# Moving the steps of the sample's key list on TensorE, and two top-k masks of the prompt into the attention

## What is computed

```python
def indexer_select(qi, wi, ki, q_pos, k_pos, n_top):
    s = jnp.einsum('bqhd,bld->bqhl', qi, ki) * IDX_DIM ** -0.5
    score = jnp.einsum('bqh,bqhl->bql', wi * IDX_HEADS ** -0.5, jax.nn.relu(s))
    score = jnp.where((k_pos[None, :] <= q_pos[:, None])[None], score, -jnp.inf)
    return lax.top_k(score, n_top)[1]
```

## Time and profile before

| | us |
|---|---|
| median of 3 runs | 1556.02 (1554.37 to 1559.13) |
| profiled execution | 1564.1 |
| its span | 1562.4 |
| PE busy | 1503.9 (96%) |
| DVE busy | 925.2 (59%) |
| POOL busy | 605.4 (39%) |
| ACT busy | 561.3 (36%) |

### The profile page before, as it was taken

One profiled execution on the slowest core, in us unless ns is written; L12 is line 12 of the kernel. 1 busy time (PEld: TensorE's weight loads), 2 busy tenths in 40 slices (PEclk: granted clock), 3 DMA queues, 4 the chain that ended last, 5 costly groups with the idle time before them and its releaser, 6 DMA issues.

```text
span 1562.4 us, 26182 instructions
## 1 busy us (share of the span) xinstructions
PE 1503.9 (96%) x9681; PEld 1388.8 (89%) x9681; DVE 925.2 (59%) x2173; ACT 561.3 (36%) x1131; POOL 605.4 (39%) x535
## 2 busy tenths in 40 slices
PE   6998999899989999998999999999999999999997
PEld 5874799569966678998998999999999999999997
DVE  5427987869987764324459555555455454555546
ACT  4325476132226653223236231422413224132233
POOL 4112393443444212111116553734627346264350
PEclk9999999999989999999999999999999999999999
DMA  7364111243100013220112110201102112021002
GB/s 220 104 184 185 35 30 28 68 136 122 41 14 2 2 42 108 85 66 28 32 50 82 55 55 27 81 27 54 54 27 81 40 40 69 12 81 54 27 9 114
DMA packets 101494, 100.30 MB, mean 64 GB/s; under 512 B 18278, under 2 KB 91638, under 8 KB 100893
## 3 DMA queue, kind: packets, MB, share of 16 engines
q1 hardware_dynamic: 93607, 88.14, 17.8%
q0 software_dynamic: 2688, 8.39, 1.7%
q10 hardware_dynamic: 5118, 2.69, 0.6%
HBM read 86.75 MB, written 12.68 MB: 64 GB/s over the span
## 4 chain that ended last, share of the span: by engine, by line
PE 59%; DVE 1%; POOL 1%; issue 1%; ACT 0%; POOLq 0%; DVEq 0%
PE banks L2072 28%; PE banks L2169 16%; PE banks L109 14%; DVE yo L2646 0%; PE banks L2029 0%; PE banks L2010 0%; PE banks L2186 0%; POOL wL L2220 0%; ACT XH L2288 0%; POOL hnL_lo L2233 0%; DVE hnL_hi L2501 0%; POOL dL L2217 0%; POOL T4L L2233 0%; ACT sH L2281 0%; ACT resid L2285 0%
## 5 line engine op out<-in xcount | busy, mean ns | idle before, releaser
L2220 POOL TENSOR_TENSOR wL<-w_raw,wH 128x512 fp32r<-128x512 f32 x176 | 231.2, 1330 | 315.1 <-ACT wH L2331 313.9
L2072 PE MATMUL banks<-hnH,wH 128*128 128x344 f32 x704 | 225.8, 321 | 2.1 <-POOL wL L2220 0.8
L2072 PE MATMUL banks<-hnH,wL 128*128 128x344 f32 x704 | 224.7, 319 | 0.0
L2633 DVE TENSOR_TENSOR resid<-resid,banks 128x344 f32<-128x344 f32 x264 | 131.9, 511 | 96.9 <-PE banks L2169 96.9
L2169 PE MATMUL banks<-aH,dH 128*128 128x344 f32 x528 | 169.3, 321 | 0.0
L2169 PE MATMUL banks<-aH,dL 128*128 128x344 f32 x528 | 169.1, 320 | 0.0
L2169 PE MATMUL banks<-aL,dH 128*128 128x344 f32 x528 | 168.2, 319 | 0.0
L1529 DVE TENSOR_SCALAR_CACHE_REDUCE pta<-SC,thr 128x512 uint8<-128x512 f32 (+4 forms) x160 | 144.0, 930 | 2.3 <-POOL SC L978 0.2
L2331 ACT ACTIVATE wH<-w_raw 128x512 fp32r<-128x512 f32 x176 | 109.6, 626 | 73.3 <-PE banks L2072 40.5
L2072 PEld LDWEIGHTS banks<-hnH,wH 128*128 128x128 f32 x704 | 132.1, 188 | 3.2 <-issue 1.8
L2072 PEld LDWEIGHTS banks<-hnH,wL 128*128 128x128 f32 x704 | 132.3, 188 | 0.0
(11 more groups left out here) (422 smaller groups left out, 3699.4 us busy)
## 6 DMA issues: line engine op xcount, KB each, us to landing
w_raw<-in_w_gate_up_dram SPq DMA_DIRECT2D x22, 1024.0 KB, 5.0
d_raw<-in_w_down_dram SPq DMA_DIRECT2D x11, 1024.0 KB, 4.8
big<-in_w_in_dram SPq DMA_DIRECT2D x11, 512.0 KB, 3.8
ZL<-x_lows SPq DMA_DIRECT2D x2, 2064.0 KB, 12.6
XL<-x_lows SPq DMA_DIRECT2D x2, 2064.0 KB, 8.5
W<-in_x_prompt_dram SPq DMA_DIRECT2D x8, 512.0 KB, 5.6
x_lows<-xnL SPq DMA_DIRECT2D x8, 512.0 KB, 3.6
slab_raw<-in_w_in_dram SPq DMA_DIRECT2D x8, 512.0 KB, 3.8
```

Source lines behind the costliest of these rows:

```text
L2072: last = mm(out, W_[w][s][:, i * P:(i + 1) * P], x_of(x)(i), start=start and i == 0 and j == 0, stop=stop and i == HALF - 1 and j == 2)
L2220: gp.tensor_tensor(wL[s].rearrange("p (k n) -> p k n", k=HALF), quadrant(x, *HOME[name]), f32(wH[s]).rearrange("p (k n) -> p k n", k=HALF) ...
L2633: V.tensor_tensor(resid[:, m, chunk(DOWN_ORDER[o])], resid[:, m, chunk(DOWN_ORDER[o])], ps[:, 4 + n % 4, 0:CH], ALU.add).then_inc(y_done, 1)
```

## The change

On TensorE the tie sums of the sample stand ahead of the last slab chunk, `sum_lanes` ahead of the pooling map, `turn_ranks` after its first group, `own_key_logits` after its third, and `list_keys` ahead of chunk 1 of L818 instead of chunk 4. On VectorE the mask of block 5 is made with those of blocks 2 to 4, ahead of the sample's softmax, and both late masks are made in ten steps, one behind each of the attention's pairs 0 to 9.

```diff
                     if x == 5:
                         pe.wait_ge(bias_row, NBUCKETS)
                         tr(ps[:, 7, 0:32], R[0:32, P - 1:2 * P - 1], ident[0:32, 0:32]).then_inc(sm_made, 1)
+                    if x == 23:
+                        pe.wait_ge(stT_evac, 1)
+                        sum_sample_ties()
                     slab_chunk(x)
...
-                pe.wait_ge(stT_evac, 1)
+                sum_lanes()
                 pe.wait_ge(uT_evac, 1)
-                sum_sample_ties()
                 pe.wait_ge(poolw_in, 16)
...
-                    if g == 1:
-                        sum_lanes()
+                    if g == 0:
+                        turn_ranks()
+                    if g == 2:
                         own_key_logits()
-
-                turn_ranks()
                 pe.wait_ge(ap_evac, NG * NCH)
...
-                before = {4: [list_keys], 7: [begin_sample_logits],
+                before = {1: [list_keys], 7: [begin_sample_logits],
...
-                for k, i in enumerate((2, 3, 4)):
+                for k, i in enumerate((2, 3, 4, 5)):
                     to_mask(k, i)
...
-                to_mask(3, 5)
                 dve.wait_ge(mask_ready, 4)
...
-                for k, i in ((4, 6), (5, 7)):
-                    for step in range(5):
-                        late_mask(k, i, step)
                 dve.wait_ge(mask_ready, 4)
                 dve.wait_ge(merged, 3 * KD)
...
+                    if n < 10:
+                        late_mask(4 + n // 5, 6 + n // 5, n % 5)
                 out_block(NBLK - 1)
```

## The result

The changed kernel takes 1571.75 us (median of 4 runs, 1569.11 to 1571.96), the one before 1555.19 beside it: ratio 1.0106, interval 1.0092 to 1.0121, so 1.06% slower: +16.6 us, interval +14.3 to +18.8. The profiled execution took 1569.11 us (span 1567.4). Forecast were 1562 and at most 1567: the direction was right, the size was not.

What follows compares the result with a forecast made beforehand. TensorE, busy almost end to end, was taken as the bound, through its stands and half clock. Front +7.7, start -5.3 and steps +5.0 gave +7.4 us on 1554.9: forecast 1562 us, own range 1558 to 1567, overall range 1551.5 to 1567.

Steps and rivals of the forecast that it cites:

- Ten steps inside the attention: Late-mask steps behind pairs 0 to 9: 15.9 us of VectorE work less 11.0 idle, taken as +5.0 us, bounds 2.2 to 8.
- upper bound: For the ten late-mask steps: 8 us, if half of VectorE's idle time in the first ten pairs can't be used.
- The two places by the order: Ahead of the row minimum and of the reciprocal of the row sums: the steps cost some 2 and 2.5 us there.
- rival D: Slower still: holes between attention pairs keep TensorE at 1.2 GHz through block 2, about 6 us more, 1568; chance 0.10.
- lower bound's 13.2: Late masks' work in the attention shrinks to 13.2 us without GpSimd arithmetic beside them, so the ten steps cost 2.2 us.
- Front, +7.7: TensorE up to the gates' end: 1.2 us around the pooling map, 5.2 wait at list_keys, 1.3 half clock; 7.7 later.
- Start, -5.3: Start of the attention: hole ahead of the first L880 shrinks from 7.2 to 1.9 us, GpSimd then late; gain 5.3.
- Mask of block 5 free: Ahead of the sample's softmax: some 5.6 us of mask hidden in VectorE's 6.48 us wait for S_ready, cost nothing.
- The base, 1554.9: Time summed from: profiled 1564.1 us less 9.2 for the hold, taken as mostly absent in runs without a profiler.
- rival B: The hold at the key transposes is in every run, repaying the list_keys wait: 1554.2, no measurable change; chance 0.27.
- B's front of -1.5: If the hold is in every run, TensorE's front costs 7.7 - 9.2 = -1.5 us, the list_keys wait being repaid.

## Why the prediction was wrong, point by point

The step that failed is "Ten steps inside the attention": +5.0 us was put, bounds 2.2 to 8, and the runs show 11.4 to 12.2 by the stages, 11 to 13 by the ratios. With 11.8 in its place the sum is 7.7 - 5.3 + 11.8 = 14.2, where 14.0 was measured on the second chip. The result's own 16.6 (14.3 to 18.8) is 2.4 more; no run says whether that is more than scatter.

- **How it came to 5.0.** The sum took VectorE's idle time in ten pairs, 11.0 us, as room for its 15.9 us of work. Measured, 4.5 us fitted. The reading, inferred from their sizes: the idle pieces are waits of a chain (logits, row minimum, exponential, transposes, values). VectorE's timeline of the kernel with the mask alone shows their size, in brackets:

```profile
455.58 0.69 DVE L1755 TENSOR_TENSOR qT<-banks,ZR 128x512 f32<-128x512 f32 x1 [1.57 <-ACT ZR L1368]
...
457.98 0.42 DVE L1778 COPY I<-banks 128x256 f32<-128x256 f32 x1 [0.70 <-PE banks L880]
...
460.80 0.29 DVE L1728 CUSTOM_DVE_ANT_0 W<-banks,SC 128x128 f32<-128x128 f32 x1 [0.54 <-PE banks L862]
```

  A step of 1.1 to 3.2 us goes whole into one such piece; what sticks out moves TensorE, and that moves all that follows. The upper bound was also worked out wrongly: half of 11.0 us unused gives 15.9 - 5.5 = 10.4, not 8. Used was a third.
- **The two places by the order.** They were named rightly: the reciprocal behind the step after the first scan, and behind the second scan. They were priced at 2 and 2.5 us; measured were waits of 3.35 and 4.21, and more half clock, which the step left out and put into rival D. Taking the reciprocal ahead of the step gave back 5.0 of 11.8 by order alone. Keeping steps out of the block's last two pairs gave 8.3 (7.8 by the ratios), by order and a wider spread together. So where a step stands is at least 5.0 of the 11.8. The shorter scans gave 5.0 too; how far these are the same 5 us stays open.
- **Half clock.** 3.5 of the 11.8 us. Rival D (1568, chance 0.10) is nearest to the result by its number, but its mechanism gave only that part; the nearness is luck.
- **The work itself.** Some steps are longer inside the attention than ahead of it. The step L1692 of the two kernels, before and after (count, shortest, median, longest in ns, first and last start):

```profile
L1692 DVE TENSOR_SCALAR late<-SC,thr x2: 685/716/748, 444.3 to 452.0; 128x896 bf16<-128x896 f32 x1, 128x1024 bf16<-128x1024 f32 x1
```

```profile
L1692 DVE TENSOR_SCALAR late<-SC,thr x2: 1610/1627/1644, 455.4 to 472.1; 128x896 bf16<-128x896 f32 x1, 128x1024 bf16<-128x1024 f32 x1
```

  It isn't the place alone: ahead of the attention the same step took 1.21 and 1.34 us in the first profile with the mask of block 5 alone. Others became shorter (L1700 from a mean of 1431 to 1217 ns). VectorE's busy time grew by 16.3 us net, near the 15.9; the lower bound's 13.2 is refuted for these pairs.
- **Front, +7.7.** Right. From the start of slab chunk 22 to the first L739 are 8.39 us in all twelve profiles with the order of before and 9.1 in the five with the new one, 0.7 more (1.0 was put); from there to the first chunk 0.2 more, the wait at the list 5.26, half clock and the rest 1.9: 8.1, and 8.5 (5.6 to 10.7) by the runs.
- **Start, -5.3.** Right: -5.6 to -6.1 by the stages. The row minimum is released through near_add, as named. But near_add is not what sets the hole: with it out of the way the last product is what is late, and the hole is the same.
- **Mask of block 5 free.** Right. With the late masks moved as well VectorE stood idle for 17.92 us ahead of the attention. The prediction noted that the late masks needn't be moved for it, and that is what the mask alone shows: the whole gain without the cost.
- **The base, 1554.9, and rival B.** The base is right for two chips out of three and for the runs beside the result. On the first chip the hold is most likely in the timed runs (median 1563.42, profile 1563.72). The whole change was not run there, but B's front of -1.5 is contradicted by its one profile with the early list: with a part of the hold stage 1 took 182.59 us, 4.8 to 5.2 more than with the front of before, and not less. Rival B also held the same 5.0 for the steps. As for the gap of about 6.2 us that the Trainium skill states ("Runtime: NRT & Kernel Launch", section "The launch sequence"), no run here can show it: each time on record, of a profiled execution or not, is 1.7 to 1.8 us above its own span, so all are times of one kind. Nor is such a gap needed: profiled executions lie among the timed runs of their kernel, all but the first of the kernel before, which has the hold (1549.62 in 1546.49 to 1551.07, 1563.72 beside 1563.42).

## What to carry to other kernels

In this kernel the idle time of a helper engine inside a tightly coupled loop was mostly no room for work (4.5 us of 12.9 took any). Before you move work there, ask into which single gap a piece goes, what stands behind it on that engine, and who waits for that. Put such pieces behind the result that another engine needs next, or outside the loop; an engine that becomes idle ahead of the loop (17.92 us here) is where they belong. When a change is made of several edits, time them apart: here one of three was the gain, and two cost more than it gave.

## What the runs showed of the hardware that was not expected

- The hold, a stand of 7.0 to 7.2 us of TensorE toward the end of the 16 key gathers, with ScalarE waiting 10 to 11 us (put down to "remote", in one profile to "issue"), came in the profiles of three of four kernels on the first chip (in the fourth, the change with the late masks ahead, ScalarE waited 11.0 us for "remote" and TensorE has 4.0 us in four short waits in its place) and in none of the eleven on the second and third, nor in that of the result. It costs 8.4 to 8.9 us in the stage, in the fourth 6.6. The profile of the kernel before that the prediction used has it too (1564.10), though the runs beside it have a median of 1556.02. Its cause stays open.
- The same scan (128x896) took 2.62 us in the kernel before, 2.02 at the same place in the kernel with the mask alone, 3.10 in the first pairs of the attention, and 2.01 behind pair 12; L1698, on one column, took 0.15 to 1.23. Which neighbour makes the difference was not tested.
- At the start of the attention TensorE falls to 1.2 GHz even where its only holes there are of 0.55 and 2.2 us: with the mask alone the granted clock was 0.61 over the first 11.22 us, and 0.92 and 1.00 in the next two windows.
